# A TensorE loop over the expert groups, written out as four copies

## The reference, cut to what matters

```python
def _hier_moe(h, wg, bg, we, be, w1, w3, w2):
    t = h.reshape(B * S, D)                      # 256 tokens of 1024
    ...                                          # top-1 group of 4, top-2 of its 4 experts
    for e in range(N_EXPERTS):                   # 16 experts, 1024 -> 512 -> 1024
        he = jax.nn.silu(t @ w1[e]) * (t @ w3[e])
        out = out + gates[:, e:e + 1] * (he @ w2[e])

for layer in range(2):
    ...                                          # mixer
    x = x + g_f * _hier_moe(h, ...)
```

## Time and profile before

| | |
|---|---|
| median of 3 runs | 1060.45 us (1057.33 to 1066.19) |
| profiled execution, its own time | 1063.53 us |
| span of its trace | 1062.0 us |
| mean granted TensorE clock | 0.908 |
| PE busy | 875.7 us (82%) |
| chain that ended last: PE, issue, DMA | 73%, 5%, 5% |

### The profile page before, as it was taken

How to read it: one execution, slowest core, us unless ns; L and a number is a source line. 1 busy time by engine, 2 the same in 40 slices (tenths; PEclk the granted TensorE clock), 3 DMA queues, 4 the chain that set the end, 5 groups by cost and what they waited for, 6 DMA issues and landing times.

```text
span 1062.0 us, 12795 instructions
## 1 busy us (share of the span) xinstructions
PE 875.7 (82%) x5253; PEld 493.7 (46%) x5254; DVE 308.7 (29%) x752; ACT 192.0 (18%) x304; POOL 144.1 (14%) x213
## 2 busy tenths in 40 slices
PE   3799386889979999799467689859999999799991
PEld 1357153475526555365245444353444463554630
DVE  1410823442203132031279911153100121211214
ACT  1301251133112131121020001022000211212110
POOL 2201004408534443300000000000000000000000
PEclk9899786968999999999878989968999999899995
DMA  9998759400999999998596484210787489799951
GB/s 311 350 381 262 259 210 361 162 2 24 394 396 348 401 396 395 396 386 345 228 330 238 160 315 160 105 54 2 247 302 241 158 308 395 290 400 391 393 196 61
DMA packets 126297, 285.48 MB, mean 269 GB/s; under 512 B 7092, under 2 KB 8388, under 8 KB 125992
## 3 DMA queue, kind: packets, MB, share of 16 engines
q1 hardware_dynamic: 119392, 276.83, 71.1%
q0 software_dynamic: 1984, 5.21, 1.6%
q10 hardware_dynamic: 4872, 2.72, 1.0%
HBM read 279.50 MB, written 5.24 MB: 268 GB/s over the span
## 4 chain that ended last, share of the span: by engine, by line
PE 73%; DVE 12%; issue 5%; DMA 5%; ACT 3%; SPq 2%; DVEq 0%; ACTq 0%
PE PS L1506 18%; PE PS L1525 12%; PE PS L1533 8%; PE PS L1549 6%; PE PS L1757 5%; PE PS L1509 5%; PE PS L1281 4%; DMA work<-in_ada_w 3%; PE PS L1476 3%; PE PS L1369 3%; DVE work L1246 2%; DMA ring<-in_ada_w 2%; PE PS L1306 2%; SPq L325 2%; PE PS L1562 1%
## 5 line engine op out<-in xcount | busy, mean ns | idle before, releaser
L1525 PE MATMUL PS<-ring,work 128*64 128x512 f32 (+1 forms) x512 | 130.5, 597 | 6.2 <-ACT work L725 6.2
L1506 PE MATMUL PS<-ring,hT 128*64 128x256 f32 x896 | 107.1, 380 | 1.6 <-DVE yg L1160 1.6
L1506 PE MATMUL PS<-ring,yg 128*64 128x256 f32 x896 | 106.7, 379 | 0.0
L1533 PE MATMUL PS<-work,xhat 128*128 128x256 f32 (+1 forms) x256 | 80.4, 471 | 20.4 <-issue 20.4
L1506 PEld LDWEIGHTS PS<-ring,hT 128*64 128x64 f32 x896 | 67.9, 137 | 36.4 <-issue 10.8
L1525 PEld LDWEIGHTS PS<-ring,work 128*64 128x64 f32 (+1 forms) x512 | 43.1, 143 | 85.4 <-issue 85.4
L1506 PEld LDWEIGHTS PS<-ring,yg 128*64 128x64 f32 x896 | 68.6, 137 | 28.1
L1171 DVE TENSOR_TENSOR work<-work,PS 128x512 f32<-128x512 f32 x32 | 22.0, 687 | 194.9 <-PE PS L1506 146.1
L1533 PEld LDWEIGHTS PS<-work,xhat 128*128 128x128 f32 x256 | 52.4, 218 | 52.2 <-issue 35.1
L1549 PE MATMUL PS<-yg,grow 64*128 64x512 f32 (+1 forms) x256 | 70.1, 612 | 7.1 <-DVE yg L1175 7.1
L1175 DVE COPY yg<-PS 128x512 f32<-128x512 f32 x32 | 22.1, 691 | 180.5 <-PE PS L1525 180.5
(11 more groups left out here) (325 smaller groups left out, 1000.2 us busy)
## 6 DMA issues: line engine op xcount, KB each, us to landing
ring<-in_moe_w SPq DMA_DIRECT2D x96, 2048.0 KB, 15.9
ring<-in_ada_w SPq DMA_DIRECT2D x19, 2048.0 KB, 13.7
work<-in_ada_w SPq DMA_DIRECT2D x5, 2048.0 KB, 16.4
ring<-in_s_glu_w SPq DMA_DIRECT2D x4, 2048.0 KB, 16.7
ring<-in_ab_w_in SPq DMA_DIRECT2D x3, 2048.0 KB, 24.3
ring<-in_ab_w_out SPq DMA_DIRECT2D x2, 2048.0 KB, 9.6
rot_tables<-work POOLq DMA_DIRECT2D x16, 256.0 KB, 5.8
ring<-rot_tables SPq DMA_DIRECT2D x2, 2048.0 KB, 11.0
```

The lines of the kernel that those rows point to most:

```text
L1506: last = mm(dst[64 * u:64 * u + 64, 0:256], hg[k][:, e * P:e * P + 64], w[:, k, 256 * u:256 * u + 256], start=k == 0, stop=k == KD - 1)
L1525: last = mm(dst, heT[:, at:at + (64 if narrow else P)], w[:, c4, h * HALF:(h + 1) * HALF], start=c4 == 0, stop=c4 == KF - 1)
L1533: last = mm(bank[k % 2].rearrange("p (e n) -> p e n", n=P)[:, :, 0:n_s], xhat[:, b, k * P:(k + 1) * P], pick[:, b, :, 0:n_s], start=b == 0 ...
```

## The change

TensorE's loop over the groups becomes a Python loop, so that the built program holds four copies of the narrow and the wide form, one pair behind the other, for each layer. The register `i` becomes a constant in each copy, and with it every semaphore value and the place of the flag in `rti`. The other engines' streams are the same as before, row for row.

```diff
                 pe.wait_ge(S("grow_ready"), n + 1)
-                with pe.Fori(0, NG) as i:
+                for i in range(NG):
                     gi, e0 = 4 * L + i, 16 * L + 4 * i
...
-                    is_narrow = pe.value_load(rti[0:1, bass.ds(i + 2, 1)], min_val=0, max_val=1)
+                    is_narrow = pe.value_load(rti[0:1, i + 2:i + 3], min_val=0, max_val=1)
                     for narrow, branch in ((True, is_narrow > 0), (False, is_narrow < 1)):
                         with pe.If(branch):
                             gather(narrow)
```

## The result

The written-out kernel takes 1078.88 us (median of 4 runs, 1075.46 to 1085.5). The kernel before, run beside it, takes 1058.89 (1051.04 to 1066.19). The ratio is 1.0194, with a 95% interval of 1.0138 to 1.025: 20 us slower, clear of noise.

The account below looks back on a forecast made before the run. The prediction took TensorE to bound the passes, with weight transfers only just keeping up. Its terms, -1.8 + 14.6 + 6.1 + 3.3 - 2.7 = +19.5 us on a median of 1060.45, gave 1080 us, range 1068 to 1093.

Parts of the forecast that it names:

- The reading of "issue": Gathers at pass starts idle while TensorE's jump fetches missing code: about 6.2 us, against 0.2 us when it is there.
- (a): Loop count, jump back and computed flag address go: 0.6 us back in each of three slow turns, -1.8 us.
- (b): Every narrow-to-narrow turn jumps into new code and is slow: two more slow turns at 7.3 us each, +14.6 us.
- (c): Skip after each layer's last narrow pass turns slow: +6.1 us in the first layer, +3.3 us in the second.
- (d): Second layer's end: the stall after the first closing matmul goes as the landing shifts within its packet, -2.7 us.
- A: Rival: the loop's jump back throws the fetcher off, so straight code loses the three slow turns; 1037 us, chance 0.06.
- B: Rival: an alternating state keeps half the skips fast in straight code; -4 to +5 us, 1056 to 1065 us, chance 0.10.
- C: Rival: landings near a packet's end add second stalls, or reading ahead and demand collide; 1093 us, chance 0.12.
- the highest sum: Upper bound of the forecast's terms, with busy stalls of 6.3 us and clock loss of 2.3 us: +31 us.

Follow-up runs that it names:

- x1: The written-out kernel with the never-taken wide form left out of the first layer: 1064.2 us, ratio 1.0071 to the kernel before.
- x2: The kernel before, with its loops, with the wide form left out of the first layer: 1054.95 us, ratio 0.9977.
- x4: The written-out kernel with the first layer's never-taken wide copies cut, giving skips of 66, 330, 388 and 330 instructions: 1077.91 us, one execution.
- v3: The written-out kernel with each pass cut in five pieces, narrow and wide in turn, so all turn jumps are short: 1042.36 us, ratio 0.9816.
- v1: The written-out kernel with each form's last scatter in an If pair of its own, so the long jump issues earlier: 1055.49 us, ratio 0.9985.
- p64: The kernel before with 64 unused semaphore increments at the head of TensorE's stream, shifting later code: 1059.8 us, one execution.
- x3: The kernel before with the loop written out in the first layer only, kept in the second: 1062.21 us, ratio 1.0038.
- p128: The kernel before with 128 unused semaphore increments at the head of TensorE's stream, shifting later code: 1042.12 us, one execution.
- p192: The kernel before with 192 unused semaphore increments at the head of TensorE's stream, shifting later code: 1064.99 us, one execution.
- v4: The kernel before, with its loops, with each pass cut in five pieces, narrow and wide in turn: 1041.81 us, ratio 0.9832.

## Why the prediction was right

**The time.** 1080 us were forecast and 1078.88 measured, +19.5 against +20.0. The profiles allow a check by terms: passes +4.3 and +6.9 us, gaps behind them +6.1 and +3.4, the stall inside the closing matmuls -2.8 (its 2.68, and the tail by the rest). That is +17.9 of the 20.0; the other two are within the spread of runs. So the mechanism and the sizes of the terms were right to about 2 us, and an agreement to half a microsecond is luck.

**The reading of "issue"** as code not on the core held. x1 and x2 took the first layer's jumps away and their stalls went; x4 gave jumps of equal length 0.33 and 6.68 us from two places; v3 made all jumps short and no stall was left between the passes. That a jump out of the packets at hand forces a fetch is also what the Trainium skill, Runtime: NRT & Kernel Launch, section "Instruction fetch mechanics", states. Its advice that follows, full unrolling, is what cost 20 us here, and the fast jumps back (0.25 us in the earlier trace rows, 0.21 to 0.25 us in all 45 of the runs here, each over a whole loop body) speak against the two blocks that it names. The same section of the Trainium skill gives TensorE 128 KiB for instructions, in blocks of 16 KiB, and that does not conflict with them.

**(a) The loop's bookkeeping**: 0.6 us forecast for a late turn; the gap ahead of the gathers went from 5.9 to 6.2 down to 5.1 to 5.3, 0.8 on the mean. Sized a little low.

**(b) Every narrow-to-narrow turn slow**: five of five are. With (a) I gave +12.8 us to the passes and they cost +11.2. The difference is (a), and the clock: the passes that begin cold and end well took 64.47 and 64.60 us, 1.3 to 1.5 over 63.15 where I had taken 2.0. But a cold start does not always cost less than before. The gathers of the second and the third pass, in the form of the earlier trace rows:

```profile
312.00:322.60 10.60, 9.52 (x32) 6.75 (x32) 0.85 1.04 400
381.66:392.95 11.29, 10.34 (x32) 7.46 (x32) 0.77 1.04 400
```

The third pass took 70.48 us and the third of the second layer 70.83, so 2.3 and 2.6 over the 68.19 of a pass with the stall alone. The idle stretches ahead of all of them are alike (5.1 to 5.3 us), so their length does not explain which start gets 0.85 and which 0.77; that stays open.

**(c) The exits**: +6.1 and +3.3 forecast, +6.1 and +3.4 measured. Pricing each by its neighbour under the same load of transfers was right: the DMA share was 1.00 during the first layer's exit (6.35 us) and 0.02 during the second's (3.74).

**(d) The 2.68 us stall** is gone, as the row of the closing matmuls shows. By the prediction's count it needed a landing just ahead of a packet's end, and the landing had moved. x1, v1 and p64 had such a stall in other places (2.32, 4.12 and 4.49 us).

**The rivals.** A (the loop throws the fetcher off) falls with x2: the first layer's loop, with jumps back and no long skip, had no stall. B (half of the skips stay fast in straight code) falls with eight slow of eight. C is a real mechanism and did not strike here; in x1, v1 and p64 it did, once each. Two slips in the sums do not move the forecast: the low end of B, -4, takes no exit as slower, while with one of them, as B says, it is -1; and the highest sum leaves out the 0.6 us of (a), with which it is +30.

**What was right only for this pair.** The prediction took the kernel before as it stood, with three slow turns, and said that it could not read by which rule the store loses code. The shifts show that this number is luck: over x2, x3 and the three shifts the second layer's loop had none, one or two slow turns. The kernel before (585.9 us of passes) was near the unlucky end. Against the luckiest loop (p128, 571.4 us of passes) the written-out passes (597.1) would have lost 26 us, against the unluckiest (p192, 587.3) 10. The rule by which such a loop loses a packet stays open.

## What to carry to other kernels

When TensorE waits for "issue" behind a branch, look at the branch's own duration and at the instruction packets before anything else: a jump to code that is not there costs about 6 us under traffic. Writing a loop out does not help if each copy must jump over an alternative; keep alternatives short and side by side, or issue the long jump while the queue still holds work. And compare variants of such a kernel stage by stage, since moving all code by 128 instructions (p128) spared this one two slow turns, 7 to 8 us each.

## What was not expected of the hardware

The price of a missed jump goes by the traffic. At a DMA share of 0.96 to 1.06 during the jump, it took 5.7 to 7.7 us in all runs here, mostly 6.1 to 6.3; at a share of 0.02, 3.3 to 3.9. Most of the difference is waiting: the packet of code started to move 3.7 us behind the jump of 310.0 in the kernel before and 1.0 us behind that of 718.3, and took 1.1 and 1.4 us to arrive. A landing shortly before the end of a packet can cost a second stall, of 2.3 to 4.5 us here. Sixty-four packets in place of 32 for the same work cost nothing that the passes show (569.4 us in v3, 570.9 in v4). And with the stalls gone, the first layer's passes run into their weights at 396 to 398 GB/s (5.3 us of waits in x1, 8.0 in v3), while the second layer's narrow passes take 63 us without such a wait.
